# A decoder trunk with a mixture of experts: FFN rows and router between the w_out groups, expert choice by ranks, constant products on a waiting TensorE

## The reference, cut to what matters

```python
y = jnp.concatenate([y_ssd, y_mla, y_moba], axis=-1) @ w_out[l]
x = x + g_m * y
hf = rms_norm(x, norm_ffn_g[l]) * (1.0 + sc_f) + sh_f
x = x + g_f * moe_ffn(hf, router_w, router_bias, w_gate[l], w_up[l], w_down[l])

# inside moe_ffn, t = the 512 rows of hf
scores = sigmoid(t @ router_w)
biased = scores + router_bias
grp = biased.reshape(-1, 4, 4)                       # 4 groups of 4 experts
group_score = sum(top_k(grp, 2)[0])                  # best group by its two best
eidx = top_k(where(in_best_group, biased, -inf), 2)  # then two experts in it
w = scores[eidx] / sum(scores[eidx])
out = sum over e: gates[:, e] * ((silu(t @ w_gate[e]) * (t @ w_up[e])) @ w_down[e])
```

## Time and profile before

| | |
|---|---|
| median of three runs | 1611.13 us (1608.15 to 1614.7) |
| the profiled execution's own time | 1612.89 us |
| its span in the trace | 1611.2 us |
| TensorE busy, mean granted clock | 1359.9 us (84%), 0.898 |
| VectorE busy | 1102.4 us (68%) |
| ScalarE busy | 720.4 us (45%) |
| GpSimd busy | 186.6 us (12%) |
| memory traffic | 379.5 MB, 236 GB/s over the span |

### The profile page before, as it was taken

One profiled execution on the slowest core, in us unless ns is written; L12 is line 12 of the kernel. 1 busy time (PEld: TensorE's weight loads), 2 busy tenths in 40 slices (PEclk: granted clock), 3 DMA queues, 4 the chain that ended last, 5 costly groups with the idle time before them and its releaser, 6 DMA issues. The chain is left out here.

```text
span 1611.2 us, 16817 instructions
## 1 busy us (share of the span) xinstructions
PE 1359.9 (84%) x6187; PEld 1051.9 (65%) x6187; DVE 1102.4 (68%) x1315; ACT 720.4 (45%) x975; POOL 186.6 (12%) x268
## 2 busy tenths in 40 slices
PE   7599987987849999999718998888794899999981
PEld 3377785656637777777506777666573777777761
DVE  0677764674558888888458786566556788888862
ACT  1423433453317766666223333345412566666640
POOL 0000014400100100000020000261010000010002
PEclk9699999688959999999858999978796899999995
DMA  9536561330538999998364374243125699999944
GB/s 342 197 107 250 168 227 53 131 108 37 225 127 328 404 406 395 395 404 328 118 225 175 130 274 161 97 152 105 66 96 229 259 386 398 401 408 401 392 149 169
DMA packets 95259, 379.52 MB, mean 236 GB/s; under 512 B 5897, under 2 KB 8695, under 8 KB 85704
## 3 DMA queue, kind: packets, MB, share of 16 engines
q1 hardware_dynamic: 71592, 308.82, 50.8%
q0 software_dynamic: 15264, 55.63, 8.9%
q10 hardware_dynamic: 8320, 13.96, 2.5%
HBM read 345.58 MB, written 32.82 MB: 235 GB/s over the span
## 5 line engine op out<-in xcount | busy, mean ns | idle before, releaser
L1022 PE MATMUL ps<-mod_rounded,work_rounded 128*128 128x512 f32 x340 | 139.7, 411 | 3.9 <-DVE work_rounded L1821 3.9
L1024 PE MATMUL ps<-mod_rounded,work_rounded 128*128 128x512 f32 x340 | 135.7, 399 | 0.0
L1705 DVE TENSOR_TENSOR ring_rounded<-ring,mod_rounded 128x2048 fp32r<-128x2048 f32 (+1 forms) x54 | 102.6, 1930 | 33.8 <-ACT mod_rounded L1311 33.8
L1705 DVE TENSOR_TENSOR work_rounded<-work,mod_rounded 128x2048 fp32r<-128x2048 f32 (+1 forms) x48 | 91.3, 1930 | 37.0 <-ACT mod_rounded L1311 37.0
L1023 PE MATMUL ps<-ring_rounded,work_rounded 128*128 128x512 f32 x288 | 114.6, 398 | 0.0
L1398 DVE SCALAR_TENSOR_TENSOR gain<-ring,csil,gain 128x512 f32<-128x512 f32 x134 | 101.8, 760 | 4.5 <-DMA ring<-in_ada_w 1.4
L1023 PE MATMUL ps<-work_rounded 128*128 128x512 f32 x256 | 101.3, 396 | 0.0
L779 PE MATMUL ps<-ring_rounded,actT_rounded 128*128 128x512 f32 (+1 forms) x256 | 93.5, 365 | 0.0
L1311 ACT ACTIVATE mod_rounded<-ring 128x2048 fp32r<-128x2048 f32 (+1 forms) x54 | 86.0, 1631 | 0.0
L1106 ACT ACTIVATE work<-x 128x1024 f32<-128x1024 f32 x16 | 16.9, 1059 | 153.7 <-DVE x L1421 80.1
L1174 ACT ACTIVATE work<-ps 128x512 f32<-128x512 f32 (+1 forms) x48 | 26.3, 549 | 129.5 <-PE ps L779 77.7
(11 more groups left out here) (325 smaller groups left out, 3546.5 us busy)
## 6 DMA issues: line engine op xcount, KB each, us to landing
ring<-in_ada_w SPq DMA_DIRECT2D x38, 1024.0 KB, 5.8
ring<-in_moe_w_gate SPq DMA_DIRECT2D x18, 2048.0 KB, 10.1
ring<-in_moe_w_up SPq DMA_DIRECT2D x18, 2048.0 KB, 10.4
ring<-in_moe_w_down SPq DMA_DIRECT2D x18, 2048.0 KB, 11.5
work<-in_moe_w_gate SPq DMA_DIRECT2D x16, 2048.0 KB, 10.1
work<-in_moe_w_up SPq DMA_DIRECT2D x16, 2048.0 KB, 10.8
work<-in_moe_w_down SPq DMA_DIRECT2D x16, 2048.0 KB, 11.5
expert_rows<-work POOLq DMA_DIRECT2D x34, 512.0 KB, 8.1
```

Source lines behind the costliest of these rows:

```text
L1022: pe.matmul(ps[j][:, :], xl, hi, start=k == 0, stop=False)
L1024: mm = pe.matmul(ps[j][:, :], xh, hi, start=False, stop=k == KD - 1)
L1705: v.tensor_tensor(slots_r[3 * odd + j][:, 512 * k0:512 * k1], slots[3 * odd + j][:, 512 * k0:512 * k1], buf.bitcast(F32), ALU.subtract).th ...
```

## The change

- TensorE: row tile t's transposes (`ffn_columns`, by halves), router and transposition back are each placed between later w_out groups; tiles 2 and 3 follow the last group. 83 products of the identity by itself into bank 7 (`keep_warm`) stand at eight places.
- VectorE: the gain is formed ahead of the first w_out sum; each row tile is x times gain before the wait for the root, then two halves of times root plus shift; the second half-group of the next tile is added behind the row tile. Expert 0's later weight parts are split after the choice.
- Choice: within each group of four an expert's rank is the number that beat it, from a 4 x 4 comparison table; the same for the groups; two experts have rank below 1.5. Comparisons without a dependence wait on one counter, `cmp_dn`.
- Ranks and totals come from one chain of 5 products; further tiles are found by VectorE (`below`, and a scan of four steps for the control words). Selectors are made by one wide comparison and one narrower one with a product, and lie in `work` instead of `actT`, so that expert 0's fourth weight part needn't wait for the table.
- After the index cast come position casts, the normalised weights, the scan and the control words. TensorE's wait for `pos_dn` stays where it was, ahead of the expert phase.
- ScalarE: exponential per tile, a silu of one column (`table_use`) behind the last one, then expert 0's weight parts.

```diff
+                def router_rows(t):
+                    pe.wait_ge(rt_ex, t + 1)
+                    pe.transpose(ps[5][:, NE * t:NE * t + NE], rt_cols, cst[0:NE, C_ID:C_ID + NE]).then_inc(rt_rows, 1)
+                def keep_warm(count):
+                    for _ in range(count):
+                        pe.matmul(ps[7][:, 0:P], ident, ident, start=True, stop=True)
...
                         mm.then_inc(acc_ps, 1)
-                to_columns(T, router)
-                pe.wait_ge(h_ev, 4 * T)
-                router(T - 1).then_inc(rt_ps, 1)
-                pe.wait_ge(rt_ex, 1)
+                        if b == 0 and t >= 2:
+                            router(t - 2)
+                        if b == 1 and t >= 2:
+                            router_rows(t - 2)
+                    if t:
+                        ffn_columns(t - 1)
+                keep_warm(9)
+                router(T - 2)
+                keep_warm(3)
+                ffn_columns(T - 1)
+                router_rows(T - 2)
+                keep_warm(2)
+                router(T - 1)
+                keep_warm(1)
+                router_rows(T - 1)
+                keep_warm(15)
+                pe.wait_ge(both_dn, 1)
+                pe.matmul(ps[5][:, 0:NE * (T + 1)], stri, both, start=True, stop=False)
                 for t in range(T):
-                    mm = pe.matmul(ps[6][0:NE, 0:1], both[:, NE * t:NE * t + NE], ones[:, 0:1],
-                                   start=t == 0, stop=t == T - 1)
+                    mm = pe.matmul(ps[5][:, NE * (t + 1):NE * (T + 1)], ones,
+                                   both[:, NE * t:NE * t + NE].unsqueeze(1).to_broadcast([P, T - t, NE]),
+                                   start=False, stop=t == T - 1)
                 mm.then_inc(rk_ps, 1)
-                pe.wait_ge(sel_dn, 2 * T)
+                keep_warm(20)
+                pe.wait_ge(sel_dn, 2)
...
+                keep_warm(28)
                 turn_x(0, 0)
+                keep_warm(5)
                 gate_up(0, 0, first=True)
...
+                        step(v.tensor_tensor(h_scaled, x[:, t, :], g_, ALU.mult))
+                        v.wait_ge(xrs, t + 2)
+                        for j in range(2):
...
+                            v.scalar_tensor_tensor(h_row(T, t).rearrange("p (k q) -> p k q", k=KD)[:, half, :],
+                                                   h_scaled.rearrange(by_k, k=KD)[:, half, :], rs_x[:, t:t + 1],
+                                                   mod[:, 3 * D:4 * D].rearrange(by_k, k=KD)[:, half, :],
+                                                   ALU.mult, ALU.add).then_inc(hrow_dn, 1)
...
+                beaten(lose, lose_flat, r3(bi, 16), 16)
+                v.wait_ge(cmp_dn, 9)
+                step(reduced(rank, lose.rearrange("p q i j -> p (q i) j")))
+                step(v.scalar_tensor_tensor(r2b, rank, 1.5, bi, ALU.is_lt, ALU.mult))
+                step(reduced(gs, r3(r2b, 16)))
+                beaten(lose_g, lose_g_flat, r3(gs, T), T)
+                v.tensor_scalar(r2m, rank, 1.5, None, ALU.is_lt).then_inc(cmp_dn, 1)
+                v.wait_ge(cmp_dn, 14)
+                step(reduced(gl, lose_g.rearrange("p q i j -> p (q i) j")))
+                v.scalar_tensor_tensor(r3(both[:, 0:T * NE], 16), bc(gl.unsqueeze(2), 16, 4), 0.5, r3(r2m, 16),
+                                       ALU.is_lt, ALU.mult).then_inc(both_dn, 1)
...
-                        v.tensor_scalar(row_oh[:, m, :], cst[:, C_IOTA:C_IOTA + P], rf[:, j, t:t + 1], None, ALU.is_equal)
-                        v.tensor_scalar(tile_tok[:, m, :], cst[:, C_IOTA:C_IOTA + NT], tf[:, j, t:t + 1],
-                                        cst[:, C_TOK + t:C_TOK + t + 1], ALU.is_equal, ALU.mult).then_inc(sel_dn, 1)
+                v.tensor_tensor(row_oh, bc(cst[:, C_IOTA:C_IOTA + P].unsqueeze(1), 2 * T, P),
+                                bc(rf.unsqueeze(2), 2 * T, P), ALU.is_equal).then_inc(sel_dn, 1)
```

More of the change, by code:

```diff
@@ L257, in trunk @@
     ss_kr = sv(596, 4)
[L259 to L275, removed]
+    route = actT[:, 0:2, :].rearrange("p a b -> p (a b)")
+    sc, bi, r2m, rank, r2b = (route[:, n:n + T * NE] for n in (0, 64, 128, 768, 832))
+    oh12 = route[:, 192:320].rearrange("p (a n) -> p a n", a=2)
+    both = route[:, 320:320 + T * NE + NE]
+    gs, gl, over = (route[:, n:n + 16] for n in (400, 416, 976))
+    lose = route[:, 448:704].rearrange("p (q i j) -> p q i j", q=T * 4, i=4)
+    lose_flat = route[:, 448:704].rearrange("p (q n) -> p q n", q=T * 4)
+    lose_g = route[:, 704:768].rearrange("p (q i j) -> p q i j", q=T, i=4)
+    lose_g_flat = route[:, 704:768].rearrange("p (q n) -> p q n", q=T)
+    w12 = route[:, 896:904].rearrange("p (a t) -> p a t", a=2)
+    wsum = route[:, 904:908]
+    j8, j1, r8, ec, base8, rf, tf, pf, t1, ctf = (
+        route[:, n:n + 8] for n in (432, 440, 912, 920, 928, 936, 944, 952, 960, 968))
+    row_oh = view(18432, 2 * T, P, of=work_r)
+    tile_tok = view(19456, 2 * T, NT, of=work_r)
+    oh_v = view(19648, 2, T * NE)
+    below = view(19776, 2 * T, NE)
+    below_n = view(17408, 2 * T, NE)
+    in_tile = view(17536, 2 * T, NT)
+    scan = [work[0:1, 17728 + 24 * n:17752 + 24 * n] for n in range(2)]
+    table_use = sv(820, 1)
+    rt_cols = prow[0:NE, :]
     cmp7 = sv(624, 112)
@@ L739, in ada_total @@
                     pe.matmul(bank[:, :], ones, ada_acc[m % 2], start=True, stop=True).then_inc(ada_ps, 1)
[L741 to L750, removed]
-                                tr = pe.transpose(h_bank(base, t, j)[:, P * k:P * k + P],
-                                                  h_row(base, t)[:, P * (4 * j + k):P * (4 * j + k) + P], ident)
-                            tr.then_inc(h_ps, 1)
-                        if behind is not None and t > 0:
-                            behind(t - 1)
@@ new lines, in _ @@
+                v.wait_ge(rk_ps, 1)
+                counts = ps[5][:, T * NE:T * NE + NE]
+                v.tensor_scalar(over, counts, float(P), None, ALU.is_gt).then_inc(cmp_dn, 1)
+                step(v.tensor_tensor(oh_v, oh12, bc(ps[5][:, 0:T * NE].unsqueeze(1), 2, T * NE), ALU.mult))
+                step(reduced(r8, oh_v.rearrange("p a (t e) -> p (a t) e", t=T)))
+                v.tensor_scalar(j1, r8, float(P), None, ALU.is_ge).then_inc(cmp_dn, 1)
+                v.wait_ge(cmp_dn, 18)
@@ L1789, in _ @@
-                step(v.scalar_tensor_tensor(pf, rf, float(NT), tf, ALU.mult, ALU.add))
-                v.tensor_copy(pos_i[:], pf).then_inc(pos_dn, 1)
-                v.wait_ge(tab_ps, 1)
-                v.tensor_copy(slot_idx[:], ps[3][:, 0:NT]).then_inc(tab_sb, 1)
+                step(v.tensor_copy(scan[0][:, 8:24], over[0:1, :]))
+                for n, shift in enumerate((1, 2, 4, 8)):
+                    src, dst = scan[n % 2], scan[1 - n % 2]
+                    step(v.tensor_tensor(dst[:, 8:24], src[:, 8:24], src[:, 8 - shift:24 - shift], ALU.add))
```

301 lines of the change are left out of this document (159 added, 142 removed).

## The result

| | before | changed |
|---|---|---|
| median of the runs, us | 1611.11 (1608.15 to 1614.7, 4 runs) | 1590.38 (1585.46 to 1592.84, 4 runs) |
| profiled execution, own time / span | 1612.9 / 1611.2 | 1589.72 / 1587.7 |
| mean granted clock of TensorE | 0.898 | 0.916 |

The mean of the changed kernel's runs is 0.9867 of the mean of before, 95% interval 0.9835 to 0.9898: a gain of 1.3%, outside the noise. The forecast was 1590.0 (1582 to 1599), faster with 0.90.

The account below looks back on a forecast made before the run. TensorE bounds the expert phase (54.0 of 54.0 us), untouched; before it, 58.9 us per layer belong to no engine for long. Segments save 10.4 per layer, 21 for two: 1612.9 becomes 1591.9, median 1.8 below, so 1590 (1582 to 1599).

Parts of the forecast that it names:

- A: Rows, columns and router, until VectorE starts on the scores: 20.2 us before, forecast to save 3.7 us per layer.
- C: Ranks on TensorE: 4.9 us before; 5 fp32 products for 14, at full clock, forecast to save 3.4 us per layer.
- D: Positions, selectors, table and index cast: 9.9 us before, 6.15 after, forecast to save 3.7 us per layer.
- E: Gather and transposes until the first gate product: 9.0 us before, 14.1 after with pause and 28 products; loses 5.1.
- B: Choosing experts, until TensorE starts the ranks: 7.4 us before, 17 operations for 30, forecast to save 3.0 us per layer.
- F: First gate half, until silu: 7.5 us before, clock up by then, forecast to save 1.7 us per layer.
- Rival 1: TensorE's clock stays up across the 3.7 us pause; E costs 3.3, the layer saves 12.2: 1586 us, chance 0.22.
- Rival 2: VectorE's new four-dimensional and broadcast operations run at the strided price; B and D lose 2.4 per layer: 1595, chance 0.13.
- Rival 3: All 28 products, the transposes and gate half run at 1.2 GHz; saves 3.5 per layer: 1604 us, chance 0.05.
- Rival 4: Slower: constant products behind the last w_out group don't hold the clock; 11.5 us later per layer: 1634, chance 0.04.
- The rule weighed against the rows: VectorE selectors: by the skill's streaming rates the replacement takes 1.07 us against 0.53, losing 0.5 per layer; rows say gain.

Follow-up runs that it names:

- experiment 7: Changed kernel with the control-word wait behind the 28 products and tile 1's router behind w_out replacing 9 constant products: 1579.96 us; run again, 1577.25 us.
- experiment 8: As experiment 7, with tile 0's router also behind w_out, odd tiles' scores in bank 6, keep_warm(3) removed: 1576.15 us, ratio 0.9772.
- experiment 6: Changed kernel with row times scale formed together with the root, behind its wait, instead of ahead of it: 1589.73 us, ratio 0.9859.
- experiment 5: Changed kernel with all tiles' transposes and routers behind w_out, no constant products among them, ScalarE's four squares ahead of the column copies: 1596.22 us, ratio 0.9894.
- experiment 3: Changed kernel with all 83 constant products left out, everything else kept: 1590.97 us, ratio 0.9848.
- experiment 1: Changed kernel with TensorE's wait for the control words moved behind the 28 constant products, all products kept: 1587.14 us, ratio 0.9829.
- experiment 2: Changed kernel without the 28 constant products behind the control words, the other 55 kept: 1583.65 us, ratio 0.9806.

## Why the prediction was right

Direction, size and way are as forecast, and the steps hold one by one (layer 0, saved per layer, forecast and measured). Experiments tested A, the clock in C and D, and E; the rest of B, C and D is read from the timelines:

| segment | forecast | measured |
|---|---|---|
| A rows, columns, router | 3.7 | 3.45 |
| B choice | 3.0 | 3.67 |
| C ranks | 3.4 | 3.48 |
| D positions to index | 3.7 | 3.60 |
| E gather, transposes | -5.1 | -5.54 |
| F gate half | 1.7 | 1.69 |
| sum | 10.4 | 10.35 |

That the sum fits to 0.05 us is luck: B saved 0.67 more than forecast, A and E together 0.69 less. So is the 0.4 us between the median and 1590, as the same kernel had a median of 1593.75 in its second group.

- **A.** The delay of w_out is 6.20 us where 5.9 was reckoned: what is drawn in is paid in full, and experiments 7 and 8 take 2.06 and 2.37 of it back. The row is ready 5.84 us after its group (5.8). That the product stands ahead of the root contributes 0.5 us to the scores (experiment 6), and the drawing in as a whole 1.4 (experiment 5). If these parts add, the remaining 1.6 of the 3.45 lies in what experiment 5 keeps too (exponentials by tile, rows in halves, the weights' low parts moved behind the rows) and was not taken apart.
- **B** was mis-sized, the only term by more than half a microsecond: eight comparisons at 0.2 us. Start to start, four of 64 and 32 values take 0.62 in all and the group ones 0.33. The 0.65 less accounts for the difference between 4.4 and the 3.79 measured.
- **C and D.** Ranks begin 1.4 us before VectorE's first step on them (1.55); the 1024-wide comparison takes 1.23 (1.22). The granted clock is 1.00 throughout, as the constant products were to make it; without them it is 0.50 there (experiment 3: 1.88 us for the table products).
- **E.** The pause is 3.91 us (3.7), the products take 8.40 (8.1), and they, not the gather, release the transposes. Half of 3.6 us was added for the slow clock; 8.40 against experiment 1's 6.50 makes it 1.9. Experiment 1 shows the mechanism: the wait alone moved, the pause and the slow clock are gone, and the layer gains 4.8 us.
- **Rival 1** (the clock survives the pause) falls by the 0.50 of 454 to 458. **Rival 2** (strided price for the new operations) falls for the choice and the selectors: the comparison with two broadcast operands runs at the plain price. A strided price shows only where the transposed view was already dear, in the two halves of 512, together 2.2 to 2.5 us where 2.1 was taken, and there it is covered. **Rival 3** (all 28 slow) would have taken 12.5 us for what took 8.40. **Rival 4** falls by the granted clock of 1.00 from 429 to 450.
- **The rule weighed against the rows.** Groups of VectorE by shape, 419 to 445 in the changed kernel:
```profile
L1772 DVE TENSOR_TENSOR actT<-actT,rbias 128x64 f32<-128x64 f32 x1 | 0.2, 225 | 0.0
...
L1792 DVE TENSOR_SCALAR actT<-actT 128x64 f32<-128x64 f32 x1 | 0.2, 188 | 0.0
```
A tensor-scalar operation on 64 values in SBUF takes 188 ns where the two-operand one takes 225. The old 16 selectors took 3.2 us start to start (460.87 to 464.08 in before, 0.2 each); the comparison of 1024 with the two 192-wide operations takes 1.15 + 0.39 + 0.36 = 1.9. So the replacement gains about 1.3 us. The Trainium skill ("VectorE: DVE Perf Modes", Side-by-side) gives tensor_scalar from SBUF two elements per cycle and fp32 tensor_tensor one; the 150 or so cycles of set-up it gives for a copy of 2048 bf16 elements, whatever the mode. By its figures (set-up, a pipe fill of 8 cycles and 32 or 64 cycles of streaming at 0.96 GHz) the two rows would be 198 and 231 ns, an estimate, and the trace agrees within 10 ns. It doesn't for the old 24-wide selectors: 285 ns in the earlier trace rows, where the same sum gives some 177. Read by streaming alone, as the prediction's sentence on it did, the rule would have made the edit a loss; with the page's own set-up term it is a gain.

What the prediction had not priced is that segment E's loss was not a condition of the gain. It priced the 28 products and the wait together, and never compared the kernel with one that lacks either: by the silus, the changed kernel without the 28 products is 3.4 us a layer faster (experiment 2), with the wait moved 4.8 (experiment 1).

## What to carry to other kernels

A wait belongs in front of the first instruction that needs what it guards; one left further ahead costs its own length and whatever the engine loses in the pause, here 4.8 us a layer. Filler that keeps the clock up must be measured against the transfer it fills: 28 products that began 3 to 4 us before the transfer landed cost 3.4 us a layer, the same 28 begun at once brought 1.3. Of work drawn into a stream that never idles take only what the end of the stream truly waits for: the early tiles' routers needn't be there, since they fitted into time that was filled with constants (experiments 7, 8); their columns should, as far as experiments 5 and 8 show it, whose scores start at 51.49 and 46.04 and which differ in the columns' place and in smaller things.

## What the runs showed of the hardware

- fp32 work behind a pause of TensorE: after 2.15 us and 2.39 us (experiment 5: eight transposes in 1.12 us, 1.04 at best) full speed; after 2.88 us, 3.82, 3.91 and 5.07 us half speed. After 2.48 us it was one in layer 0 and the other in layer 1 of one execution (experiment 3), so the length of the pause alone doesn't settle it.
- One kernel's executions differ by up to 13 us, though the changed part repeated to 0.05 us in the changed kernel's two traces and to 0.2 in the two of experiment 7. The clock elsewhere is the part that I can name. The turn from the first silu to the second takes 14.6 us or 16.2, and the long form came in both layers of experiment 1, in one layer of experiment 7 and of the kernel before, and in no other profile. With the long turn goes a dip of the granted clock (experiment 1); which of them causes the other isn't shown:
```profile
470.00:474.00 4.00, 2.98 (x18) 2.28 (x16) 4.00 (x4) 2.19 (x4) 0.75 (x1) 1.00 1.10 410
474.00:478.00 4.00, 3.33 (x11) 2.55 (x12) 3.11 (x5) 4.00 (x5) 0.29 (x1) 0.70 0.87 347
```
- Layer 1's attention had 20 us at half clock in the kernel without the 28 products, where the changed kernel had 0.69 in the like stretch (both some 20 us behind the last qkv products). The stretch of the kernel without the 28, then that of the changed kernel:
```profile
1042.00:1062.00 20.00, 19.89 (x62) 12.74 (x62) 15.83 (x32) 9.64 (x23) 1.94 (x3) 0.50 0.44 158
```
```profile
1052.00:1070.00 18.00, 16.36 (x74) 12.36 (x74) 11.70 (x30) 10.74 (x26) 5.56 (x7) 0.69 0.67 234
```
From the last qkv products to the last scores that attention took some 96 us there, 93 in experiment 1 and 88 in the changed kernel. These 5 us, of which 2 came back ahead of w_out, and the long turns (2 x 1.6 us) hide most of what experiment 1 gained: 9.5 us by its silus, 3.1 by the profiled spans. So the silus, not the medians, tell these variants apart. What decides the clock there is open; no run was made on it.
